# Turning the second half of tile 0's next input behind tile 1's last unit

## The reference

```python
# block 1, per layer                      # block 2, per layer
x = LN(ALPHA*x + 0.5*swiglu(x, ...))      x = x + 0.5*rms(swiglu(rms(x, g0), ...), g1)
x = LN(ALPHA*x + mixer(x, ...))           x = x + rms(token_mixer(rms(x, g2), ...), g3)
x = LN(ALPHA*x + 0.5*swiglu(x, ...))      x = x + 0.5*rms(swiglu(rms(x, g4), ...), g5)
```

## Time and profile before

| | |
|---|---|
| median of 3 runs | 2111.23 us (2110.16 to 2111.27) |
| the profiled execution, its own time | 2110.42 us |
| its span, first to last instruction | 2108.7 us |
| PE busy | 2092.6 us, 99% of the span |
| DVE busy | 1685.4 us, 80% |
| ACT busy | 1082.3 us, 51% |
| POOL busy | 80.7 us, 4% |
| granted TensorE clock | 1.00 |

### The profile page before, as it was taken

The page is one execution under the profiler, slowest core; times in us unless marked ns, Lnnn a source line. Parts: engine busy times, 40 slices in busy tenths (PEclk is TensorE's granted clock), DMA queues, the critical chain, the costliest instruction groups (busy, mean ns, idle before and its releaser), DMA issues.

```text
span 2108.7 us, 28912 instructions
## 1 busy us (share of the span) xinstructions
PE 2092.6 (99%) x10580; PEld 1776.2 (84%) x10580; DVE 1685.4 (80%) x3158; ACT 1082.3 (51%) x1568; POOL 80.7 (4%) x128
## 2 busy tenths in 40 slices
PE   9999999999999999999999999999999999999998
PEld 7888999888888899988878887988887888888887
DVE  6888766888888867778888887779888888678886
ACT  5445554544544455444454446575445445766443
POOL 0000010000000000000000001010000000101000
PEclk9999999999999999999999999999999999999999
DMA  7765755666566584557656766346665765645663
GB/s 249 235 194 175 221 168 156 188 218 191 177 218 193 176 234 143 187 168 224 196 153 213 215 190 196 126 135 208 212 197 166 225 192 168 185 140 161 211 191 106
DMA packets 314368, 395.56 MB, mean 188 GB/s; under 512 B 17972, under 2 KB 272212, under 8 KB 313972
## 3 DMA queue, kind: packets, MB, share of 16 engines
q1 hardware_dynamic: 309120, 375.52, 58.0%
q0 software_dynamic: 4944, 18.14, 2.7%
q10 hardware_dynamic: 164, 0.06, 0.0%
HBM read 392.59 MB, written 1.06 MB: 187 GB/s over the span
## 4 chain that ended last, share of the span: by engine, by line
PE 94%; DVE 3%; ACT 1%; issue 1%; DMA 0%; POOL 0%; DVEq 0%; POOLq 0%; SPq 0%; ACTq 0%
PE bank L310 26%; PE bank L312 26%; PE bank L311 26%; PE bank L304 4%; PE bank L305 4%; PE bank L306 4%; DVE w_lo L294 1%; PE bank L491 1%; PE bank L1472 1%; PE bank L1493 1%; PE bank L1002 1%; PE bank L1564 1%; ACT w_hi L287 0%; DVE xh L831 0%; DVE x L806 0%
## 5 line engine op out<-in xcount | busy, mean ns | idle before, releaser
L287 ACT ACTIVATE w_hi<-stage 128x1024 fp32r<-128x1024 f32 x711 | 746.8, 1058 | 635.4 <-PE bank L312 537.5
L294 DVE TENSOR_TENSOR w_lo<-stage,w_hi 128x1024 fp32r<-128x1024 f32 x711 | 864.8, 1224 | 213.6 <-ACT w_hi L287 206.6
L310 PE MATMUL bank<-w_hi,xt_hi 128*128 128x512 f32 x1760 | 692.0, 393 | 6.5 <-DVE xt_lo L846 5.6
L312 PE MATMUL bank<-w_hi,xt_lo 128*128 128x512 f32 x1760 | 685.5, 389 | 0.0
L311 PE MATMUL bank<-w_lo,xt_hi 128*128 128x512 f32 x1760 | 685.3, 389 | 0.0
L477 DVE STREAM_TRANSPOSE hidden<-hidden 32x128 f32<-32x128 f32 (+1 forms) x1376 | 391.7, 285 | 21.3
L310 PEld LDWEIGHTS bank<-w_hi,xt_hi 128*128 128x128 f32 x1760 | 330.5, 188 | 77.2 <-DVE xt_lo L846 4.6
L312 PEld LDWEIGHTS bank<-w_hi,xt_lo 128*128 128x128 f32 x1760 | 330.4, 188 | 69.1
L311 PEld LDWEIGHTS bank<-w_lo,xt_hi 128*128 128x128 f32 x1760 | 330.6, 188 | 66.4
L310 PE MATMUL bank<-w_hi,mt_hi 128*128 128x512 f32 x768 | 303.3, 395 | 0.2 <-DVE mt_lo L561 0.2
L312 PE MATMUL bank<-w_hi,mt_lo 128*128 128x512 f32 x768 | 299.4, 390 | 0.0
(11 more groups left out here) (279 smaller groups left out, 1387.5 us busy)
## 6 DMA issues: line engine op xcount, KB each, us to landing
stage<-in_ffn_w SPq DMA_DIRECT2D x352, 256.0 KB, 3.2
stage<-in_ffn_w_in SPq DMA_DIRECT2D x352, 256.0 KB, 3.2
stage<-in_ffn_w SPq DMA_DIRECT2D x88, 512.0 KB, 3.7
stage<-in_ffn_w_out SPq DMA_DIRECT2D x88, 512.0 KB, 3.7
stage<-in_w_in SPq DMA_DIRECT2D x80, 512.0 KB, 3.9
stage<-in_mix_w_in SPq DMA_DIRECT2D x56, 512.0 KB, 4.2
stage<-in_w_out SPq DMA_DIRECT2D x16, 512.0 KB, 4.2
stage<-in_mix_w_out SPq DMA_DIRECT2D x16, 512.0 KB, 3.5
```

The costliest lines, as they stand in the source:

```text
L287: act.activation(w_hi[:, u % RING, :], stage[:, u % STAGED, :], ACT.Copy).then_inc(S["hi_ready"], 1)
L294: dve.tensor_tensor(w_lo[:, u % RING, :], stage[:, u % STAGED, :], f32(w_hi[:, u % RING, :]), ALU.subtract).then_inc(S["lo_ready"], 1)
L310: pe.matmul(o, m_hi, hi, start=first, stop=False)
L312: return pe.matmul(o, m_lo, hi, start=False, stop=last)
```

## The change

In all three kinds of stage, PE turns half 0 of tile 0's next input ahead of tile 1's last unit as before, and half 1 behind that unit. On DVE, the rest of one unit more (unit 4 of the next stage) is formed behind, and no longer ahead of, `xt_lo` of tile 0 at the ends of FFNs; and tile 1's variance behind an FFN is formed once unit 4's rest is done, with unit 5's rest behind it, where it stood behind unit 5's rest. Behind `mix1` and `mix2` DVE's order stays as it was (the lines there are only rewritten).

```diff
 # pe_ffn, the last LAG units of tile 1 (pe_out_proj and pe_mix2 alike)
                 if turn and v == n - 1:
-                    pe_turn_x(pe, s + 1, 0)
+                    pe_turn_half(pe, s + 1, 0, 0)
                 pe_ffn_tile(pe, s, 1, v)
                 pe_turn_hidden(pe, s, 1, v)
+            if turn:
+                pe_turn_half(pe, s + 1, 0, 1)
 # dve_ffn, start of a stage
                 dve_norm_start(dve, s - 1, 1)
-                if STAGES[s - 1] == "mix2":
-                    dve_norm_var(dve, s - 1, 1)
+                if STAGES[s - 1] != "mix2":
+                    lo_upto(dve, b + (5 if STAGES[s - 1] == "ffn" else 6))
+                dve_norm_var(dve, s - 1, 1)
                 lo_upto(dve, b + 6)
-                if STAGES[s - 1] != "mix2":
-                    dve_norm_var(dve, s - 1, 1)
                 dve_norm_x(dve, s - 1, 1)
 # dve_ffn, end of a stage
                 dve_pre_x(dve, s + 1, 0)
-                lo_upto(dve, b + n + 5)
+                lo_upto(dve, b + n + 4)
                 dve_xt(dve, s + 1, 0)
 # dve_mix1 (dve_mix2 alike)
             dve_norm_start(dve, s - 1, 1)
+            lo_upto(dve, base + 5)
+            dve_norm_var(dve, s - 1, 1)
             lo_upto(dve, base + 6)
-            dve_norm_var(dve, s - 1, 1)
             dve_norm_x(dve, s - 1, 1)
```

## The result

The changed kernel takes 2120.77 us (median of 4 runs, 2120.08 to 2121.83) against 2111.15 for the kernel before (4 runs, 2110.16 to 2111.27). The ratio is 1.0045, 95% interval 1.0033 to 1.0057. I had forecast +3.8 us, and it is +9.6. The profiled execution took 2120.08 us, its span is 2118.3.

The account below looks back on a forecast made before the run. The prediction took PE, busy 99% of the span, as the bound. Its terms by ends, -0.6 + 0.8 + 0.7 + 0.2 + 2.7 = +3.8 us, gave 2115.0 us, with its own range 2112.7 to 2117.3 and a wider one 2110.7 to 2117.3.

Parts of the forecast that it names:

- What bounds the kernel: PE, busy for 99% of the span; the change can only take away or add time in which PE stands.
- unit prices: Step costs read from the trace: four transposes 0.40 us, a one-tile unit 1.36, behind transposes 1.45, a rest 1.14.
- part 1: Half 1 turned behind the last unit: 1.36 us later at every end, making tile 1's norm and turn late.
- Ends 2, 5, 8 and 11: Ends behind a mixer: +0.41 us each at 2 and 5, +1.4 each at 8 and 11, from half 1's lateness.
- Part 2: Unit 4's rest behind `xt_lo` at FFN ends: `xt_lo` starts as ACT allows; at end 1 the wait goes, 0.80 us won.
- Rival (c): Much slower: delayed weight loads make PE wait at seven ends, +12.2 us, 2123.4; chance 0.07.
- Part 3: Variance ahead of unit 5's rest at FFN ends: variance to x takes 1.26 us instead of 0.88, 0.38 more.
- Rival (d): The clock falls to half behind new gaps of about 1.6 us at ends 8 and 11: +17 us, 2128.6; chance 0.01.
- (a): Faster: tile 1's norm keeps its slack and PE's seven gaps just close, -6.6 us, 2104.6; chance 0.07.
- (b): No change: FFN ends keep some 0.7 us of their gains, offsetting the mixer ends' +3.5, 2111.2; chance 0.11.

Follow-up runs that it names:

- e1: The kernel before with PE's change alone (half 1 turned behind the last unit in all three kinds of stage), DVE's order unchanged: 2115.04 us, ratio 1.0016.
- e5: The kernel before with PE's change only at the ends behind `mix1` and `mix2`: 2114.90 us, ratio 1.0015.
- e2: The changed kernel with PE's turn of both halves back ahead of the last unit, so DVE's change alone: 2106.78 us, ratio 0.9976.
- e9: The changed kernel with unit 5's rest at the seven FFN ends made in two instructions of 512 columns: 2115.45 us, ratio 1.0019.
- e4: The changed kernel with eight matmuls, results unused, added ahead of tile 1's turn at end 6 alone: 2118.64 us, ratio 1.0031.
- e3: The changed kernel with unit 5's rest at the FFN ends taking its minuend from PSUM, not SBUF (values wrong): 2115.00 us, ratio 1.0015.
- e10: The changed kernel with tile 1's variance behind unit 5's rest again at the seven FFN ends: 2122.07 us, ratio 1.0052.
- e6: The changed kernel with PE's order behind `mix1` and `mix2` as before, the seven FFN ends changed whole: 2116.43 us, ratio 1.0022.

## Why the prediction was wrong, point by point

**What bounds the kernel, the unit prices and part 1: right.** Half 1 is 1.83 later than half 0 (1.85), and what suffers is tile 1's norm, not unit 2.

**Ends 2, 5, 8 and 11: right, +3.5 forecast.** By ends it is +3.5 in the changed kernel, in e1 and in e5. The chain without a hole in the earlier trace rows was the safest evidence in the profile.

**Part 2: right.** `xt_lo` starts as ACT allows, and the 7 waits are gone (e2, changed kernel). Rival (c), late loads, did not show: no waits for `w_lo` at units 4 to 10 appeared.

**Part 3: the step that failed.** I put from variance to x at "0.12 + 1.14 = 1.26", with POOL's power hidden under unit 5's rest, at the 0.55 that it takes while DVE waits for it. It is 1.79, because the power takes 1.47 beside that rest. By the difference of the changed kernel and e9 this is 0.5 to 0.7 at each of six FFN ends (0.48, 0.55, 0.59, 0.67, 0.53, 0.52, together 3.3) and some 0.5 of end 6. The mechanism stood in the trace of before: the same power on one value per partition, L820, runs there beside the rests of the next units. Timeline of the kernel before, at end 6:

```profile
1106.45 3.48 DVE L294 TENSOR_TENSOR w_lo<-stage,w_hi 128x1024 fp32r<-128x1024 f32 x3
...
1106.61 1.46 POOL L820 TENSOR_TENSOR scale<-var,neg_half 128x1 f32<-128x1 f32 x1 [5.71 <-DVE var L815]
```

The prediction took POOL's price from the places where DVE waits for it, and moved it to a place where DVE is at work.

**Rival (d): right in kind, at the wrong end.** I had looked for the fall of the clock behind the new stands of 1.6 us at ends 8 and 11. It stayed at 1.00 there (1.58). At end 6, where my sums had PE come 1.1 us earlier and x 0.63 later on top of a stand of 0.20, I never added up the stand. They make 1.9; without part 3's miss it is 1.66 (e9), as PE comes 0.8 earlier and not 1.1. Part 3's miss lengthened it to 2.19, and there the clock fell, at a cost of 1.6 us (e4). The sum had both at nothing. (I had also written that the trace of before shows only the upper level. In its last 2 us, with PE idle, it shows less: 0.68 over 2106 to 2108.)

**The sum.** +3.8 forecast, 3.3 and 0.5 for part 3 and 1.6 for the clock make 9.2, the table's sum. Without the first cause the second did not arise in the traces of e9 and e3, and the changed kernel comes to 2115.45 (e9) and 2115.00 (e3), where I had put it at 2115.0. Rivals (a) and (b) were wrong for this kernel, yet e2 is what (a) looks like once PE's half of the change is left out.

## What to carry to other kernels

The price of an instruction that is moved under other work is that of a row where it runs beside such work; a row where its consumer waits for it idly shows another. When a small operation is to be hidden behind a long one on another engine, look whether both need SBUF in a way that shuts one out, and if so cut the long one, or let it read one operand from PSUM (e3 shows what that gives in time; its data were others). And when several terms each lengthen PE's stand at one place, add up the stand itself: behind the 2.19 and 2.42 us here the clock went down as well, and that cost three times what the longer stand itself did (1.6 against 0.5).

## What the runs showed of the hardware

POOL's power of 128x1 values takes 0.55 to 0.57 alone or beside a DVE subtraction with one input in PSUM, 1.46 to 1.47 beside a DVE subtraction of 1024 columns with both inputs in SBUF, and 0.93 beside two of 512. The second half was not held up in turn: both together took 1.28 us, as the two halves of `xt_lo` do, although the power was still running when it began.

That the power is let in behind the first subtraction is not certain where a second one follows at once. At the place of L820 three or four rests stand in a row, six times in each of the twelve traces. In 70 of these 72 rows the power takes 1.46, in two (one in e1, one in e10) 3.7, that is until 0.41 behind the third and last rest. DVE and ACT did not wait for it there. Timeline of e10 at end 9:

```profile
1620.09 3.49 DVE L294 TENSOR_TENSOR w_lo<-stage,w_hi 128x1024 fp32r<-128x1024 f32 x3
...
1620.25 3.73 POOL L821 TENSOR_TENSOR scale<-var,neg_half 128x1 f32<-128x1 f32 x1 [5.59 <-DVE var L816]
```

PE's clock stayed at 1.00 behind stands of 1.58 (ends 8 and, in e3, 6), 1.66 (e9) and 1.76 and 1.77 us (e10, ends 7 and 10), and fell to 0.50 behind 2.19 (changed kernel, e6) and 2.42 (e10), in each case for some 3 us of work. That the length of the stand alone decides is not shown: e6's three runs with a mean clock of 1.000 speak against it, unless their stand was shorter, which no trace of them shows.
